# Token lists of experts 32 to 63 filled from the other end of the partitions

## The chip, the cores and the metric

The kernel runs on one core of a Trainium2 chip. Its engines are TensorE (PE, with its weight loads as PEld), VectorE (DVE), ScalarE (ACT), GpSimd (POOL) and SyncE (SP); SP, ACT and POOL also issue transfers, which sixteen DMA engines of the core carry out. The metric is the device time of one execution in microseconds, as the median of several runs.

## What is computed

One layer of a hybrid encoder on 512 tokens of width 1024: a mixer (a state space branch and a windowed attention branch), then a mixture of experts, then a norm. The change is in the routing of the mixture:

```python
scores = jax.nn.sigmoid((n @ router_w).astype(jnp.float32))
biased = scores + router_bias.astype(jnp.float32)
...
_, eidx = lax.top_k(jnp.where(emask, biased, -jnp.inf), TOP_K)
w = jnp.take_along_axis(scores, eidx, axis=-1)
w = w / jnp.sum(w, axis=-1, keepdims=True) * ROUTE_SCALE
...
for e in range(N_EXPERTS):
    hid = jax.nn.silu(n @ e_gate[e]) * (n @ e_up[e])
    out = out + (hid @ e_down[e]) * combine[:, e:e + 1]
```

There are 64 experts of hidden width 256 and one shared expert; each token goes to 6 of the 64, so 3072 rows (token and expert) are computed. All is float32.

## The kernel before

Up to about 590 us of the span the kernel does the mixer. Then the routing runs over four tiles of 128 tokens, mingled with the output projection of the mixer and with the shared expert, and from about 645 us on the experts.

**Lists.** For each token tile DVE chooses the six experts (`choose`, L1396 to L1405), PE counts with a triangular matrix how many rows of each expert came before (`positions`, L1956 and L1957), and DVE turns that into a slot for each of the six rows (`places`, L1420 to L1431). POOL then writes the entry of each row (token, weight, row number) with an indirect transfer to that slot of the table `list_d` in HBM (`list_tile`, L714, six transfers per tile; it waits for `ordered`, which `places` raises). An entry's place n in its expert's list gives its block, n / 64, and within the block its partition, 4 (n mod 16) + n / 16: sixteen entries in a row go to sixteen groups of four partitions, the next sixteen to the second partition of each group, and so on. Slots that no entry fills hold a number that is out of bounds, for which the indirect transfers move nothing. For expert 0 alone the list is also made by PE (`list_of_first`, L1448 to L1455 on DVE, L2014 on PE), so that its rows can be gathered before the table is read back. DVE then ranks the experts by length (L1484 to L1492) for the order in which they are loaded.

**Units.** The experts run in 42 units. The four first experts and the sixteen longest lists have a unit each (up to 128 rows: one block in the lower 64 partitions, one in the upper), the others share one in pairs (64 rows each, one expert per half). For each unit POOL gathers the rows of the normed tokens from HBM into `xs` (L754, one indirect transfer, one row of 4 KB per filled partition), PE turns them (L2020), ACT and DVE apply the modulation, PE does gate and up (`gate_up`, L2032), ACT and DVE the activation, PE the down product (`down`, L2040), DVE scales the result (L1510) and POOL scatters the rows to `expert_rows` in HBM (L767). PE does gate and up of a unit before the down product of the unit before.

**Weights.** An expert's weights are three transfers of 1 MB: gate (L517), up (L518) and down (L521), all issued by SP in the order of use. There are six slots. A slot's gate and up halves are loaded again when the gate and up products of the expert in it are done (`gu_ready`), its down half after its down product (`ey_ready`).

**Tail.** When all scatters have landed (L578), SP reads the six rows of each token (L582), and DVE and PE add them, DVE norms and SP stores.

On PE the order around the routing is written by hand: `shared_gu(0)`, `turn_h(3)`, `positions(2)`, part of `shared_gu(1)`, `router(3)`, the rest, `positions(3)` (waits for `choose(3)` on DVE), the row counts (L2061), `shared_gu(2, 1 to 5)`, `list_of_first` (waits for DVE's L1455), `shared_gu(2)`, `shared_turn(0)`, the ranks (L2068), `shared_gu(3)`, the turn of the first unit's rows, the rest of the shared expert, and the units. On DVE `places(2)` stands ahead of `shared_hid(0)` (L1444) and `best_two(3)` (L1378), and `places(3)` ahead of L1448. In DVE's code `chain(...)` makes the next instruction wait for the one inside.

Of the kernel before, what the change touches and what calls it, by code (L numbers as in the profile page):

```python
# [5 lines left out]
ALU = mybir.AluOpType  # L6
# [6 lines left out]
P = 128  # L13
SEQ = 512
D = 1024
T = SEQ // P
# [25 lines left out]
NE = 64  # L42
TOPK = 6
RGROUPS = 8
# [7 lines left out]
HALF = P // 2  # L52
STRIPE = 16
# [43 lines left out]
def hybrid_ssd_swa_moe_adaln_block(nc, a):  # L97
# [58 lines left out]
    with ExitStack() as ctx:  # L156
# [50 lines left out]
        with ExitStack() as own:  # L207
# [27 lines left out]
            slot = tile(own, "slot", [P, T, TOPK], U32)  # L235
# [69 lines left out]
        def dn(s):  # L305
# [24 lines left out]
        fin_g = xsT[:, 0, :, :].rearrange("p k c -> p (k c)")  # L330

        widths = [KC * NE, NE, TOPK * NE, NE, RGROUPS * 8, RGROUPS * RGROUPS, RGROUPS * RGROUPS, P, RGROUPS * RGROUPS,
                  NE, NE, NE, T * RGROUPS, T * 8, T * 8, T * TOPK, T * TOPK, P, T, T * 4, T * TOPK * 4, 2 * T * TOPK]
        routing = xsT[:, :, :, :].rearrange("p b k c -> p (b k c)")
        spans = [routing[:, sum(widths[:i]):sum(widths[:i + 1])] for i in range(len(widths))]
        r_w = spans[0].rearrange("p (k e) -> p k e", k=KC)
# [7 lines left out]
        nth_of, place0 = spans[17], spans[18]  # L344
        entry0 = spans[19].rearrange("p (t w) -> p t w", t=T)
        parts0 = spans[20].rearrange("p (t w k) -> p t w k", t=T, w=4)
        whole = spans[21].rearrange("p (t w k) -> p t w k", t=T, w=2)
        gs, top8, indf, s6, p6 = (spans[i].rearrange("p (t w) -> p t w", t=T) for i in range(12, 17))

# [680 lines left out]
        def _(dve):  # L1030
            steps = [0]

            def chain(ins):

                steps[0] += 1
                ins.then_inc(dve_step, 1)
                dve.wait_ge(dve_step, steps[0])
# [380 lines left out]
            def places(t):  # L1418
# [5 lines left out]
                dve.tensor_scalar(whole[:, t, 0, :], p6[:, t, :], -(STRIPE - 1) / 2, 1.0 / STRIPE, ALU.add, ALU.mult)  # L1424
                chain(dve.tensor_scalar(whole[:, t, 1, :], p6[:, t, :], -(HALF - 1) / 2, 1.0 / HALF, ALU.add, ALU.mult))
                dve.tensor_scalar(whole[:, t, :, :], whole[:, t, :, :], ROUND, -ROUND, ALU.add, ALU.add)
                chain(dve.scalar_tensor_tensor(out=p6[:, t, :], in0=p6[:, t, :], scalar=float(NE * HALF // STRIPE),
                                               in1=indf[:, t, 0:TOPK], op0=ALU.mult, op1=ALU.add))
                chain(dve.scalar_tensor_tensor(out=p6[:, t, :], in0=whole[:, t, 0, :], scalar=float(NE * (1 - HALF)), in1=p6[:, t, :],
                                               op0=ALU.mult, op1=ALU.add))  # L1430
                dve.scalar_tensor_tensor(out=slot[:, t, :], in0=whole[:, t, 1, :], scalar=float(NE * (HALF - HALF // STRIPE)),  # L1431
                                         in1=p6[:, t, :], op0=ALU.mult, op1=ALU.add).then_inc(ordered, 1)

            def add_shared(t):
                if t == 0:
# [752 lines left out]
```

## Time and profile before

| | us |
|---|---|
| median of 3 runs | 1208.58 |
| lowest and highest | 1207.26, 1210.27 |
| the profiled execution | 1209.25 |
| its span, first to last instruction | 1207.2 |
| PE busy | 1148.4 (95%) |
| DVE busy | 539.6 (45%) |
| POOL busy | 197.0 (16%) |
| DMA: 334.71 MB moved | mean 277 GB/s |

The span is cut into 40 slices of 30.2 us on the page of the profile. A group of instructions is named by the line of kernel.py that issued it, its engine and what it writes and reads. Idle time stands in brackets, with the engine, tile and line that ended it. The DMA share of a window is the mean of the packets' time over sixteen engines; it can be a little over 1, since packets overlap. Instructions issued by a queue's sequencer carry a q (SPq).

### The profile page before, as it was taken

To read this page: it belongs to the slowest core of one execution; us is meant where nothing else is said; L and a number is where in the kernel's file an instruction comes from. 1 tells how busy PE (TensorE), PEld (TensorE's weight loads), DVE (VectorE), ACT (ScalarE), POOL (GpSimd) and SP (SyncE) were. 2 spreads that over 40 slices of the span, in tenths; PEclk is the share of its full clock that TensorE was granted. 3 is DMA by queue.
4 is the path that set the end of the run, shared out by engine and by line. 5 is a ranking of instruction groups with operands and counts; after the bars stand their busy time and mean duration, and the time that the engine had idled before them with its cause. 6 is when DMAs were issued, how large, how long until landed. Compare 5 with 4: busy or idle time off the path is not lost. (4 is left out here: it accounts for less than half of the span.)

```text
span 1207.2 us, 13966 instructions
## 1 busy us (share of the span) xinstructions
PE 1148.4 (95%) x4935; PEld 654.0 (54%) x4935; DVE 539.6 (45%) x1160; ACT 254.6 (21%) x635; POOL 197.0 (16%) x326
## 2 busy tenths in 40 slices
PE   4999999998999999999999999999999999989885
PEld 2545875565566888889754444444444443433332
DVE  5673123555666777635764222222232222222156
ACT  2131222233442111101211111212121121111101
POOL 5000010112011010010441212121212122111101
PEclk9999999999999999999999999999999999999898
DMA  9942142233578365275447999999999999999996
GB/s 301 261 140 69 35 141 70 71 105 135 201 277 323 128 184 166 87 282 233 149 162 270 345 420 422 423 423 423 422 423 421 422 422 423 421 422 422 422 363 262
DMA packets 111212, 334.71 MB, mean 277 GB/s; under 512 B 14580, under 2 KB 67912, under 8 KB 84136
## 3 DMA queue, kind: packets, MB, share of 16 engines
q1 hardware_dynamic: 88048, 269.39, 57.4%
q0 software_dynamic: 21568, 59.68, 13.8%
q10 hardware_dynamic: 1528, 4.77, 1.0%
q8 instruction: 39, 0.64, 0.2%
q14 instruction: 29, 0.24, 0.1%
HBM read 314.51 MB, written 38.35 MB: 292 GB/s over the span
## 5 line engine op out<-in xcount | busy, mean ns | idle before, releaser
L2032 PE MATMUL ps<-gu_hi,xsT 128*64 128x512 f32 (+1 forms) x704 | 239.1, 613 | 14.5 <-DMA gu_hi<-in_exp_w_up_dram 6.9
L2032 PEld LDWEIGHTS ps<-gu_hi,xsT 128*64 128x64 f32 (+1 forms) x704 | 83.0, 154 | 124.6 <-issue 123.2
L1514 DVE SCALAR_TENSOR_TENSOR hid<-ps,wgt,gated 128x256 f32<-128x256 f32 x42 | 20.3, 483 | 280.2 <-ACT gated L1004 280.2
L2032 PE MATMUL ps<-gu_lo,xsT 128*64 128x512 f32 (+1 forms) x320 | 141.1, 594 | 1.9 <-issue 1.0
L2040 PE MATMUL ps<-dn_hi,hidT 128*64 128x512 f32 (+1 forms) x352 | 119.9, 597 | 1.1 <-DVE hn L1510 1.1
L1659 PE MATMUL ps<-n1T,ring 128*128 128x512 f32 x256 | 111.8, 593 | 0.0
L767 POOL DMA_INDIRECT expert_rows<-hn,meta x40 | 40.0, 1000 | 368.1 <-DVE hn L1510 327.7
L1510 DVE TENSOR_TENSOR hn<-ps,g_row 128x1024 f32<-128x1024 f32 x42 | 51.4, 1224 | 91.0 <-PE ps L2040 90.8
L1004 ACT ACTIVATE gated<-ps 128x256 f32<-128x256 f32 x42 | 16.1, 384 | 306.1 <-PE ps L2032 306.1
L1659 PEld LDWEIGHTS ps<-n1T,ring 128*128 128x128 f32 x256 | 48.2, 190 | 58.4 <-issue 58.4
L2032 PEld LDWEIGHTS ps<-gu_lo,xsT 128*64 128x64 f32 (+1 forms) x320 | 49.9, 161 | 51.9 <-issue 51.6
L2040 PE MATMUL ps<-dn_lo,hidT 128*64 128x512 f32 (+1 forms) x160 | 72.5, 596 | 0.0
L994 ACT ACTIVATE xsT<-ps,mod 128x128 f32<-128x128 f32 x172 | 64.8, 457 | 27.8 <-PE ps L2020 27.8
L2040 PEld LDWEIGHTS ps<-dn_hi,hidT 128*64 128x64 f32 (+1 forms) x352 | 38.7, 150 | 48.1 <-issue 46.2
L1504 DVE TENSOR_SCALAR xsT<-ps,mod 128x128 f32<-128x128 f32 x172 | 58.7, 403 | 6.5 <-PE ps L2020 6.5
L2020 PEld LDWEIGHTS ps<-ident,hn 128*128 128x128 f32 x344 | 42.9, 191 | 30.5 <-issue 27.5
L1844 PE MATMUL ps<-xbcT,ring 128*128 128x512 f32 x128 | 58.4, 599 | 0.0
L1668 PE MATMUL ps<-ring,n1T 128*128 128x256 f32 x256 | 57.6, 386 | 0.0
L1924 PE MATMUL ps<-ring,raw 128*128 128x256 f32 x256 | 56.6, 380 | 0.9 <-issue 0.9
L1668 PEld LDWEIGHTS ps<-ring,n1T 128*128 128x128 f32 x256 | 49.1, 193 | 7.5 <-issue 0.7
L1924 PEld LDWEIGHTS ps<-ring,raw 128*128 128x128 f32 x256 | 48.1, 190 | 7.5 <-issue 1.2
L754 POOL DMA_INDIRECT hn<-norm_rows,meta x44 | 46.1, 1047 | 34.5 <-issue 32.1
(387 smaller groups left out, 1531.1 us busy)
## 6 DMA issues: line engine op xcount, KB each, us to landing
gu_hi<-in_exp_w_gate_dram SPq DMA_DIRECT2D x44, 1024.0 KB, 25.4
gu_hi<-in_exp_w_up_dram SPq DMA_DIRECT2D x44, 1024.0 KB, 28.8
dn_hi<-in_exp_w_down_dram SPq DMA_DIRECT2D x44, 1024.0 KB, 28.9
ring<-in_w_in_dram SPq DMA_DIRECT2D x20, 1024.0 KB, 6.1
gu_lo<-in_exp_w_gate_dram SPq DMA_DIRECT2D x20, 1024.0 KB, 26.2
gu_lo<-in_exp_w_up_dram SPq DMA_DIRECT2D x20, 1024.0 KB, 29.6
dn_lo<-in_exp_w_down_dram SPq DMA_DIRECT2D x20, 1024.0 KB, 29.5
h<-in_ada_w_dram POOLq DMA_DIRECT2D x32, 512.0 KB, 4.9
```

The lines of the kernel that those rows point to most:

```text
L754: pool.indirect_dma_start(out=xs[:, b, :], out_offset=None, in_=norm_d[:, :], in_offset=bass.IndirectOffsetOnAxis(ap=meta[:, c, 0:1], axis=0),
L767: pool.indirect_dma_start(out=rows_d[:, :], out_offset=bass.IndirectOffsetOnAxis(ap=meta[:, c, 1:2], axis=0), in_=ys[:, b, :], in_offset=N ...
L994: ins = act.activation(xsT[:, b, k, :], ps[:, 0, P * k:P * k + P], ACT.Identity, bias=B2[:, k:k + 1], scale=A2[:, k:k + 1])
L1504: ins = dve.tensor_scalar(xsT[:, b, k, :], ps[:, 1, P * (k - 4):P * (k - 4) + P], A2[:, k:k + 1], B2[:, k:k + 1], ALU.mult, ALU.add)
L1510: dve.tensor_tensor(ys[:, b, :], flat(ps[:, 5:7, :]), g2_row[:, :], ALU.mult).then_inc(ey_dve, 1)
L1659: ins = pe.matmul(bank, w[:, k, lo:lo + P], n1T[:, k, :], start=(k == 0), stop=(k == KC - 1))
L1668: ins = pe.matmul(bank[:, 0:cols], n1T[:, k, P * t:P * t + P], w[:, k, :], start=(k == 0), stop=(k == KC - 1))
L1844: ins = pe.matmul(ps[:, 1, :], w[:, k, P * (m % 2):P * (m % 2) + P], uT[:, k, :], start=(k == 0), stop=(k == KC - 1))
L1924: ins = pe.matmul(ps[:, 2 * (t % 2) + b // 2, WB * (b % 2):WB * (b % 2) + WB], mergedT[:, k, P * t:P * t + P], w[:, k, :], start=(k == 0), ...
L2020: ins = pe.transpose(ps[:, k // 4, P * (k % 4):P * (k % 4) + P], xs[:, b, :].rearrange("p (f k) -> p k f", k=KC)[:, k, :], ident[:, :])
L2032: ins = pe.matmul(ps[rows, 2 + b, :], xsT[:, b, k, rows], gu(s)[:, :, k, :], start=(k == 0), stop=(k == KC - 1))
L2040: ins = pe.matmul(ps[rows, 5 + half, :], hidT[:, jj, rows], dn(s)[:, jj, BANK * half:BANK * half + BANK], start=(jj == 0), stop=(jj == 1))
```

## The change

The slots of experts 32 to 63 are mirrored within each half of 64 partitions: an entry that went to partition p of its block goes to 63 - p. The slot is p x 64 + e + 4096 x block; the old code made it with three instructions out of the place, the two rounded quotients (`whole`: place / 16 and place / 64) and the expert's number. The new code forms the partition with a factor of 1 or -1 (`turned_round`, first a mask of experts from 32 up) and adds a base (`base_of`) that is the expert's number for the others and includes the far end of the block for the turned ones. Six instructions more per token tile, all on 128 x 6 elements.

```diff
-                  NE, NE, NE, T * RGROUPS, T * 8, T * 8, T * TOPK, T * TOPK, P, T, T * 4, T * TOPK * 4, 2 * T * TOPK]
+                  NE, NE, NE, T * RGROUPS, T * 8, T * 8, T * TOPK, T * TOPK, P, T, T * 4, T * TOPK * 4, 2 * T * TOPK, TOPK, TOPK]
...
+        turned_round, base_of = spans[22], spans[23]
...
                 dve.tensor_scalar(whole[:, t, :, :], whole[:, t, :, :], ROUND, -ROUND, ALU.add, ALU.add)
-                chain(dve.scalar_tensor_tensor(out=p6[:, t, :], in0=p6[:, t, :], scalar=float(NE * HALF // STRIPE),
-                                               in1=indf[:, t, 0:TOPK], op0=ALU.mult, op1=ALU.add))
-                chain(dve.scalar_tensor_tensor(out=p6[:, t, :], in0=whole[:, t, 0, :], scalar=float(NE * (1 - HALF)), in1=p6[:, t, :],
-                                               op0=ALU.mult, op1=ALU.add))
-                dve.scalar_tensor_tensor(out=slot[:, t, :], in0=whole[:, t, 1, :], scalar=float(NE * (HALF - HALF // STRIPE)),
-                                         in1=p6[:, t, :], op0=ALU.mult, op1=ALU.add).then_inc(ordered, 1)
+                chain(dve.tensor_scalar(turned_round, indf[:, t, 0:TOPK], float(NE // 2), None, ALU.is_ge))
+                dve.tensor_scalar(base_of, whole[:, t, 1, :], float(2 * HALF * NE), float((HALF - 1) * NE), ALU.mult, ALU.add)
+                chain(dve.scalar_tensor_tensor(out=p6[:, t, :], in0=whole[:, t, 0, :], scalar=-float((HALF - 1) * STRIPE) / HALF,
+                                               in1=p6[:, t, :], op0=ALU.mult, op1=ALU.add))
+                dve.tensor_tensor(base_of, base_of, turned_round, ALU.mult)
+                chain(dve.scalar_tensor_tensor(out=p6[:, t, :], in0=whole[:, t, 1, :], scalar=float(STRIPE - 1),
+                                               in1=p6[:, t, :], op0=ALU.mult, op1=ALU.add))
+                dve.tensor_tensor(base_of, base_of, indf[:, t, 0:TOPK], ALU.add)
+                chain(dve.tensor_scalar(turned_round, turned_round, -2.0, 1.0, ALU.mult, ALU.add))
+                chain(dve.tensor_tensor(p6[:, t, :], p6[:, t, :], turned_round, ALU.mult))
+                dve.scalar_tensor_tensor(out=slot[:, t, :], in0=p6[:, t, :], scalar=float(NE * HALF // STRIPE), in1=base_of,
+                                         op0=ALU.mult, op1=ALU.add).then_inc(ordered, 1)
```

DVE, places(3), before. `xsT` is the buffer in which all small routing tiles lie; `dve_step` is the semaphore of `chain`, `counted` is raised by PE.

```order
L1420 TENSOR_TENSOR xsT<-dn_hi,ps 128x384 [waits counted]
L1423 TENSOR_REDUCE xsT<-xsT 128x6 [waits dve_step]
L1424 TENSOR_SCALAR xsT<-xsT 128x6 [waits dve_step]
L1425 TENSOR_SCALAR xsT<-xsT 128x6
L1426 TENSOR_SCALAR xsT<-xsT 128x12 [waits dve_step]
L1427 SCALAR_TENSOR_TENSOR xsT<-xsT 128x6
L1429 SCALAR_TENSOR_TENSOR xsT<-xsT 128x6 [waits dve_step]
L1431 SCALAR_TENSOR_TENSOR slot<-xsT 128x6 [waits dve_step]
L1448 SCALAR_TENSOR_TENSOR xsT<-ps,dn_hi 128x4
```

The same place after the change, from the rounding on (lines are up to seven higher from here on):

```order
L1427 TENSOR_SCALAR xsT<-xsT 128x12 [waits dve_step]
L1428 TENSOR_SCALAR xsT<-xsT 128x6
L1429 TENSOR_SCALAR xsT<-xsT 128x6 [waits dve_step]
L1430 SCALAR_TENSOR_TENSOR xsT<-xsT 128x6
L1432 TENSOR_TENSOR xsT<-xsT 128x6 [waits dve_step]
L1433 SCALAR_TENSOR_TENSOR xsT<-xsT 128x6
L1435 TENSOR_TENSOR xsT<-xsT 128x6 [waits dve_step]
L1436 TENSOR_SCALAR xsT<-xsT 128x6
L1437 TENSOR_TENSOR xsT<-xsT 128x6 [waits dve_step]
L1438 SCALAR_TENSOR_TENSOR slot<-xsT 128x6 [waits dve_step]
L1455 SCALAR_TENSOR_TENSOR xsT<-ps,dn_hi 128x4
```

Three instructions have become nine, five of the nine wait for the one before, and the write of `slot` stands last in both.

PE, from positions(3) to the first matmul of `shared_gu(3)`, is the same sequence in both kernels; so it reads before:

```order
L1956 MATMUL ps<-xsT,ones 128x64 [waits ordered,routed]
L1957 MATMUL ps<-dn_hi,xsT 128x64
L2061 MATMUL ps<-xsT,ones 128x64 [waits score_done]
L2061 MATMUL ps<-dn_hi,ones 128x64
L1979 MATMUL ps<-gu_hi 128x512 [waits n2_dve,shared_in]
L1979 MATMUL ps<-gu_hi 128x512 x4
L2014 MATMUL ps<-xsT,lists 128x4 [waits o_read,list0_in]
...
L2068 MATMUL ps<-dn_hi,ecol 1x64 [waits routed]
L1979 MATMUL ps<-gu_hi 128x512 [waits ordered,shared_in]
```

Nothing moved there, but three of these waits (`ordered` and `routed` at the first row, `list0_in`, `routed` at L2068) are for DVE instructions that stand behind the changed step.

## Rows read from the trace of the kernel before

**Rows 1.** Page: busy time and share per engine; busy tenths in 40 slices.
```profile
PE 1148.4 (95%) x4935; PEld 654.0 (54%) x4935; DVE 539.6 (45%) x1160; ACT 254.6 (21%) x635; POOL 197.0 (16%) x326
DMA  9942142233578365275447999999999999999996
```

**Rows 2.** Windows: start and end, length, busy per engine, granted clock, DMA share, GB/s.
```profile
617.40:626.70 9.30, 9.30 (x26) 4.34 (x27) 2.42 (x14) 0.66 (x2) 5.91 (x7) 1.00 0.07 14
645.00:650.00 5.00, 5.00 (x13) 2.25 (x12) 2.33 (x2) 0.00 (x0) 0.00 (x0) 1.00 0.56 210
650.00:655.00 5.00, 3.70 (x18) 2.13 (x19) 2.05 (x7) 2.17 (x6) 0.31 (x2) 1.00 0.44 131
660.00:665.00 5.00, 5.00 (x23) 2.50 (x20) 1.85 (x5) 1.89 (x5) 0.00 (x0) 1.00 0.46 166
665.00:1148.00 483.00, 467.19 (x1811) 202.94 (x1809) 129.65 (x315) 89.09 (x235) 94.45 (x159) 0.99 1.02 417
800.00:1146.00 346.00, 333.85 (x1298) 144.73 (x1296) 90.59 (x221) 63.30 (x167) 66.74 (x113) 0.98 1.02 422
```

**Rows 3.** Waits of PE, 690 to 1165 us: total, times, longest; and one such wait.
```profile
PE ps L2032 <- DMA gu_hi<-in_exp_w_up_dram: 7.8, 3, 3.6
PE ps L2032 <- DMA gu_lo<-in_exp_w_up_dram: 3.9, 2, 3.1
...
1118.71 9.65 PE L2032 MATMUL ps<-gu_hi,xsT 128*64 128x512 f32 x32 [3.64 <-DMA gu_hi<-in_exp_w_up_dram]
```

**Rows 4.** Chain that ended last, in order of time: start, length, what.
```profile
1024.29 8.78 PE ps L2032 x32
...
1046.31 29.30 DMA gu_hi<-in_exp_w_up_dram
...
1106.31 27.73 DMA gu_hi<-in_exp_w_up_dram
...
1134.37 7.09 PE ps L2032 x32
...
1148.94 8.75 DMA expert_rows<-hn,meta
...
1157.75 0.34 SPq L582
```

**Rows 5.** Windows at the end of the weight stream, columns as in rows 2.
```profile
1146.00:1148.00 2.00, 0.56 (x4) 0.32 (x2) 1.45 (x3) 0.38 (x1) 0.00 (x0) 1.00 1.02 430
1148.00:1150.00 2.00, 0.34 (x2) 0.23 (x4) 0.00 (x0) 0.00 (x0) 1.06 (x2) 1.00 0.95 401
1150.00:1152.00 2.00, 2.00 (x12) 0.86 (x10) 0.00 (x0) 0.00 (x0) 1.24 (x3) 1.00 0.93 391
1152.00:1154.00 2.00, 2.00 (x12) 0.71 (x10) 0.00 (x0) 0.00 (x0) 0.08 (x1) 1.00 0.79 322
1154.00:1156.00 2.00, 2.00 (x12) 0.84 (x10) 0.00 (x0) 0.00 (x0) 0.00 (x0) 1.00 0.65 258
1156.00:1158.00 2.00, 2.00 (x14) 1.16 (x12) 0.61 (x2) 0.51 (x2) 0.00 (x0) 1.00 0.38 154
1158.00:1160.00 2.00, 2.00 (x12) 0.61 (x10) 1.24 (x4) 1.38 (x4) 0.00 (x0) 1.00 0.77 197
1160.00:1162.00 2.00, 1.86 (x10) 0.57 (x6) 0.46 (x1) 0.11 (x1) 0.00 (x0) 1.00 0.98 406
```

**Rows 6.** Timeline of DVE, places(3): start, length, engine, line, operation.
```profile
614.05 0.17 DVE L1424 TENSOR_SCALAR xsT<-xsT 128x6 f32<-128x6 f32 x1
614.13 0.16 DVE L1425 TENSOR_SCALAR xsT<-xsT 128x6 f32<-128x6 f32 x1
614.33 0.17 DVE L1426 TENSOR_SCALAR xsT<-xsT 128x12 f32<-128x12 f32 x1
614.41 0.16 DVE L1427 SCALAR_TENSOR_TENSOR xsT<-xsT 128x6 f32<-128x6 f32 x1
614.60 0.17 DVE L1429 SCALAR_TENSOR_TENSOR xsT<-xsT 128x6 f32<-128x6 f32 x1
614.80 0.17 DVE L1431 SCALAR_TENSOR_TENSOR slot<-xsT 128x6 uint32<-128x6 f32 x1
```

**Rows 7.** Timeline of DVE: what stands behind places(0) and places(1).
```profile
575.23 0.69 DVE L1351 TENSOR_TENSOR work<-ps,g_row 128x512 f32<-128x512 f32 x1 [2.52 <-PE ps L1924]
...
592.16 0.69 DVE L1351 TENSOR_TENSOR work<-ps,g_row 128x512 f32<-128x512 f32 x1 [2.60 <-PE ps L1924]
```

**Rows 8.** Timeline, tile 2's slots to the stream's start; window; gather's time to landing.
```profile
605.27 0.17 DVE L1431 SCALAR_TENSOR_TENSOR slot<-xsT 128x6 uint32<-128x6 f32 x1
605.35 0.42 DVE L1444 TENSOR_TENSOR lists<-ps,gated 128x256 f32<-128x256 f32 x1
605.68 0.21 DVE L1378 TENSOR_TENSOR xsT<-dn_hi,xsT 128x64 f32<-128x64 f32 x1
606.27 1.01 POOL L714 DMA_INDIRECT token_lists<-pay,slot  x1 [2.04 <-DVE slot L1431]
607.59 0.97 POOL L714 DMA_INDIRECT token_lists<-pay,slot  x1 [0.30 <-issue]
...
611.32 0.43 PE L1956 MATMUL ps<-xsT,ones 128*128 128x64 f32 x2 [0.58 <-DVE dn_hi L1405]
...
615.80 1.06 POOL L714 DMA_INDIRECT token_lists<-pay,slot  x1 [1.94 <-DVE slot L1431]
...
616.55 0.97 PEld L2014 LDWEIGHTS ps<-xsT,lists 128*128 128x128 f32 x8 [0.61 <-DVE xsT L1455]
...
619.89 1.05 POOL L754 DMA_INDIRECT hn<-norm_rows,meta  x1 [0.48 <-issue]
...
626.76 1.04 PE L2020 MATMUL ps<-ident,hn 128*128 128x128 f32 x8
...
644.68 7.03 PE L2032 MATMUL ps<-gu_hi,xsT 128*128 128x512 f32 x16
...
651.89 0.33 SPq L517 DMA_DIRECT2D gu_hi<-in_exp_w_gate_dram  x1
...
661.66 0.33 SPq L517 DMA_DIRECT2D gu_hi<-in_exp_w_gate_dram  x1
...
DMA to landing us min/median/max: 3.1/9.6/17.0
...
626.70:651.60 24.90, 24.90 (x98) 12.98 (x97) 14.30 (x30) 2.83 (x8) 5.51 (x8) 1.00 0.76 284
```

## The prediction

> **What bounds the kernel now.** I read the page of the profile first: its row of busy times says 95% for PE, and the row of the DMA engines stands at nine tenths from the middle of the span to its end [rows 1]. So two resources look full in the expert part, and the windows tell them apart. From 665 to 1148 us the DMA share is 1.02, which is what full looks like in this view; before that, at 645 to 655 and 660 to 665 us, it is 0.44 to 0.56, because the six weight slots are full and the next load must wait until PE has freed one [rows 2]. The table of waits has PE waiting 7.8 + 3.9 us for expert weights [rows 3], and the chain of waits runs over PE until 1044 us and then over two weight loads that take 29.30 and 27.73 us from issue to landing [rows 4]. A transfer of 1 MB at 422 GB/s is 2.5 us; such a load stands behind some ten others. PE has small gaps, the transfers none: from 665 us on the time is set by how much the DMA engines have to move, and by when the stream starts. The stream starts when PE has used the first expert, so PE's and DVE's time before 652 us counts, and almost nothing that PE, DVE, ACT or POOL do between 665 and 1134 us does.
>
> "The DMA engines" are sixteen, and a load has landed when the last of them is done. The windows at the stream's end show that they don't end together: the share falls from 1.02 to 0.95, 0.93, 0.79, 0.65 and 0.38 between 1148 and 1158 us, while the last scatter of rows, issued at 1148.94, lands only at 1157.69, and SP issues the reads of the tail right behind it, at 1157.75 [rows 4, 5]. Below full by 0.07, 0.09, 0.23, 0.37 and 0.64, times 2 us: the mean engine is idle for 2.8 us there. With the next two windows (0.77 and 0.98, in part the start of the new reads) it is 3.4 us. So the busiest engine ends some 2.8 to 3.4 us after the mean one, and the tail waits for the busiest.
>
> **The change, part by part: the DVE work.** It keeps three of the six instructions behind the reduction at L1423 and puts nine in the place of the other three, six more per tile. What matters is the distance of two starts. On tile 3 an instruction that waits for the one before starts 0.19 or 0.20 us after it (614.13 to 614.33, 614.41 to 614.60, 614.60 to 614.80) and one that waits for nothing 0.08 us after (614.05 to 614.13) [rows 6]. From L1426 to the write of slot that is 0.08 + 0.19 + 0.20 = 0.47 us. In the new order the starts behind the rounding are 0.08 (turned_round), 0.19 (base_of), 0.08, 0.20, 0.08, 0.20, 0.08, 0.20, 0.20 = 1.31 us. So +0.84 us for each tile.
>
> Which tiles pay? Tiles 0 and 1 end in front of an idle DVE: it waits 2.52 and 2.60 us there for the output projection [rows 7]. That covers 0.84, and POOL's list writes of these tiles are behind a queue of their own (1.3 us from start to start [rows 8], six per tile). Behind tile 2 DVE goes on at once with L1444 and L1378, and both what it reads there are ready; POOL waits for the slots of tile 2 (2.04 us) and again for those of tile 3 (1.94 us), and PE waits for DVE at positions(3), 0.58 us, and before list_of_first, 0.61 us [rows 8]. These are waits that end with DVE, so the delay passes on: 0.84 us at positions(3) and 1.68 us at list_of_first. Queued behind the waiting matmul are the shared expert, the turn of the first gathered rows and the first unit, and PE is busy without a gap from 617.4 to 651.6 us [rows 2, 8], so nothing there takes the delay up. Nor does a transfer: the DMA share is 0.07 between 617.4 and 626.7 us [rows 2]. The first gather has landed by then (POOL issues it at 619.89, and the 3.1 us that such a gather takes at the least [rows 8] are over before PE's turn at 626.76; both move alike). SP's loads into freed slots, issued at 651.89 and 661.66 us [rows 8], move with PE. The stream starts **1.7 us later**. Ends: 0, if something else ends these waits, and 4 x 0.84 = 3.4 us if all four tiles pay. I take 1.7, for the idle time in rows 7 is three times the addition and there is none behind tiles 2 and 3.
>
> **The balance.** A list's n-th entry of a block goes to partition 4 (n mod 16) + n/16 of its half; entries without a token move no row. Lists are 3 to 125 entries long on these inputs (by the reference's routing), and 60 of the 64 end within a round of 16, which leaves the higher groups of four partitions one row short. Summed over all units, the 32 groups of four partitions hold between 76 and 110 rows, mean 96; with the lists of experts 32 to 63 turned they hold between 91 and 100. A row is 4 KB and is moved twice, gathered and scattered. At 422 GB/s over sixteen engines 4 KB take 4096 / 26.4 = 155 ns [rows 2]. If an engine serves fixed partitions, one group's 14 rows above the mean are 14 x 2 x 0.155 = 4.3 us of work, and 4 rows are 1.2 us. The idle time of the tail, 2.8 to 3.4 us, is of that size, which is why I believe that it comes from the rows. The turned lists take (14 - 4)/14 = 0.71 of the excess away: 0.71 x 3.1 = **2.2 us sooner**. Ends: 0, if engines do not serve fixed partitions or their lag has another cause, and 3.4 us, all that the tail shows idle.
>
> The Trainium skill ("DMA: Bandwidth & Descriptors", section "The descriptor swizzle") states which engine writes which partitions: groups g and g+8 of a half belong to one engine. By that pairing the busiest engine has 208 rows against a mean of 192 now, and 198 then; an estimate from it is 10 x 2 x 0.155 = 3.1 us sooner, and the sum would be 1.7 - 3.1 = -1.4 us, 1207.2 us.
>
> **The sum.** The profiled execution took 1209.25 us, 1207.2 of it the span; the median of the runs is 0.67 us lower. +1.7 - 2.2 = -0.5 us: 1208.75 us for a profiled execution, 1208.1 us against the median of 1208.58. What is late next is the same engine as before: after the change the stream is still full, its last load and the last scatter still end it, and the 13 MB of reads behind it and the tail on DVE do not change.
>
> **Rivals.** (1) The cost is hidden: PE's two waits of 0.6 us are ended by something that doesn't move, or the start of the stream is set by a transfer. The nearly idle DMA engines of 617.4 to 626.7 us speak against it. 1208.58 - 2.2 = 1206.4. (2) The balance is worth nothing: all engines share one limit, and those that end first only had the smaller share. For it: the share is 1.02 whatever runs. Against it: the staircase in rows 5, with 16 equal parts in every weight load. 1208.58 + 1.7 = 1210.3. (3) Slower: the engines that serve the highest partitions are slow by themselves, and their short lists hid it. The turned lists give a high group of four 13 to 16 rows more; 13 x 2 x 0.155 = 4.0 us on that engine, and with 1.7 us of DVE 5.7 us: 1214.3. It decides as soon as that engine's own slowness is over 13 rows' worth, 4 us in 490. Rows 5 show one long staircase and no engine's name, so nothing excludes it; little speaks for it. The Trainium skill (the same page, section "Latency and other measured facts") has such a rule: engines 7 and 15 are "usually slower" than the others. By its swizzle these serve the highest groups of the two halves. No row here names an engine, so no run here shows it. (4) More than the tail: PE's stalls go too. A stall is followed by slow matmuls: behind the 3.64 us wait at 1118.71 the 32 matmuls take 9.65 us in place of 7.1 [rows 3, 4]. If that stall and its slow stretch go and PE, not the stream, then sets the last scatter, 3.6 + 2.6 us go and 1.7 us come: 1204.1. Against it: PE is given its time back only where it is the later of the two, and at 1134.37 it again waits for a load.
>
> **How the numbers follow.** Chances: the forecast 0.55 (1206.5 to 1209.7 us, the gain between 1.4 and 3.4 us and the cost between 1.4 and 2.4), rival 1 0.12, rival 2 0.13, rival 3 0.10, rival 4 0.10. The range reaches from the largest gain at no cost, 1208.58 - 3.4 = 1205.2, to no gain at the cost of four tiles with a small margin for the runs' own spread, 1211.8; outside stay rivals 3 and 4. A measurement of this kernel tells about 0.3%, 3.6 us, from no change. Faster by more than that: rival 4 and a small part of rival 1, 0.12. Slower: rival 3 and a small part of rival 2, 0.12. Within: 0.76.
>
> **What the profile after would show.** In the places step of tiles 2 and 3 the distance from L1427 to the write of slot is 1.3 us, and the first unit's L2032 (now L2039) starts near 646.4 us in place of 644.68. The first load into a freed slot is issued near 653.6 us. The DMA share is 1.02 until about 1150 us and then falls in one or two windows, not in five; the idle time summed over these windows is near 1 us in place of 2.8 to 3.4. The last scatter lands near 1157.2. I am wrong in the cost if the first unit starts within 0.5 us of its old time, and wrong in the gain if the staircase is gone and the last scatter still lands later than 1158.5, or if the staircase is as long as it was.

## The result, and the profile after

| | before | changed |
|---|---|---|
| median of 11 runs each, same chip | 1208.89 | 1212.40 |
| lowest and highest | 1205.95, 1210.27 | 1208.76, 1213.23 |
| ratio, with 95% interval | | 1.0022 [1.0014, 1.0031] |
| the profiled execution and its span | 1209.25, 1207.2 | 1208.76, 1206.6 |

The change costs 2.7 us by the ratio (1.7 to 3.7); the medians stand 3.5 us apart. 2.7 us is less than the 3.6 us that this kernel's measurement tells from no change, so by size it is the case "within 0.3%"; but the interval excludes a gain, and 1212.4 lies above the range that I gave.

The profiled execution of the changed kernel happens to be the quickest of its eleven. Its part ahead of the changed code ran 2.2 us earlier: the first matmul of the output projection stands at 527.96 us before and at 525.72 after, at the same code. So absolute times of the two traces are not to be compared; what is compared here is the distance from one event to a later one.

First the DVE work. The timeline of DVE in the changed kernel, places(3) (start, length, engine, line, operation), answers to [rows 6]:

```profile
612.90 0.17 DVE L1427 TENSOR_SCALAR xsT<-xsT 128x12 f32<-128x12 f32 x1
612.98 0.16 DVE L1428 TENSOR_SCALAR xsT<-xsT 128x6 f32<-128x6 f32 x1
613.18 0.17 DVE L1429 TENSOR_SCALAR xsT<-xsT 128x6 f32<-128x6 f32 x1
...
614.01 0.17 DVE L1437 TENSOR_TENSOR xsT<-xsT 128x6 f32<-128x6 f32 x1
614.21 0.17 DVE L1438 SCALAR_TENSOR_TENSOR slot<-xsT 128x6 uint32<-128x6 f32 x1
```

From the rounding to the write of `slot` it is 1.31 us, against 0.47. The waits around it in the changed kernel, timelines of DVE, PE, POOL and SP, answer to [rows 7, 8]:

```profile
573.02 0.69 DVE L1352 TENSOR_TENSOR work<-ps,g_row 128x512 f32<-128x512 f32 x1 [1.69 <-PE ps L1931]
...
604.86 1.01 POOL L715 DMA_INDIRECT token_lists<-pay,slot  x1 [2.11 <-DVE slot L1438]
...
609.90 0.43 PE L1963 MATMUL ps<-xsT,ones 128*128 128x64 f32 x2 [1.62 <-DVE dn_hi L1406]
...
651.28 0.33 SPq L518 DMA_DIRECT2D gu_hi<-in_exp_w_gate_dram  x1
```

DVE's idle time behind tile 0 has shrunk from 2.52 to 1.69 us, by just the addition: there it is hidden. PE's wait for DVE at positions(3) has grown from 0.58 to 1.62 us. The write of the first slots (571.16 us) comes 1.38 us earlier than before, the first load into a freed slot only 0.61 us earlier (651.28 against 651.89), and the part ahead of both is 2.24 us earlier: 1.63 us are lost on the way.

So from the first matmul of the output projection to the first load into a freed slot it is 123.93 us before and 125.56 after.

Then the stream's end. Windows of the changed kernel, columns as in [rows 2], answering to [rows 5]:

```profile
1148.00:1150.00 2.00, 0.43 (x2) 0.23 (x4) 0.00 (x0) 0.00 (x0) 1.18 (x3) 1.00 1.02 430
1150.00:1152.00 2.00, 2.00 (x12) 0.86 (x10) 0.00 (x0) 0.00 (x0) 1.19 (x3) 1.00 0.98 412
1152.00:1154.00 2.00, 2.00 (x12) 0.81 (x10) 0.00 (x0) 0.00 (x0) 0.00 (x0) 1.00 0.83 336
1154.00:1156.00 2.00, 2.00 (x12) 0.75 (x10) 0.00 (x0) 0.00 (x0) 0.00 (x0) 1.00 0.48 180
1156.00:1158.00 2.00, 2.00 (x14) 1.16 (x12) 0.70 (x2) 0.60 (x2) 0.00 (x0) 1.00 0.57 131
1158.00:1160.00 2.00, 2.00 (x12) 0.70 (x10) 1.15 (x4) 1.29 (x4) 0.00 (x0) 1.00 0.84 332
```

The staircase is shorter at its top: the share stands at 0.98 until 1152, so the engines that used to be done first now work longer. It is not gone: the share still falls to 0.48. And the last weight load lands when it did. The group of the last load's issue, before and then changed (the time to landing is that of the last of sixteen engines):

```profile
L521 SPq DMA_DIRECT2D dn_lo<-in_exp_w_down_dram x1: 498/498/498, 1133.5 to 1133.5; - x1
...
DMA to landing us min/median/max: 26.2/26.2/26.2
```

```profile
L522 SPq DMA_DIRECT2D dn_lo<-in_exp_w_down_dram x1: 679/679/679, 1133.2 to 1133.2; - x1
...
DMA to landing us min/median/max: 26.4/26.4/26.4
```

1133.5 + 26.2 = 1159.7 us before and 1133.2 + 26.4 = 1159.6 after, though the stream started 0.6 us earlier: 507.8 us after the first load into a freed slot before, 508.3 us after it now. The last scatter of rows landed 505.8 us after that load before and 505.1 us now (at 1156.35 us). The chain of waits of the changed kernel no longer goes over it, but over the last up load and PE:

```profile
1118.01 31.22 DMA gu_lo<-in_exp_w_up_dram
1149.57 7.09 PE ps L2039 x32
1157.74 3.61 PE ps L2047 x16
1161.73 24.14 DMA gu_hi<-expert_rows
```

**A measure for all runs.** Each of these loads raises its semaphore sixteen times, and the trace holds those times; I take them for the landings on the sixteen engines. From them I took, for the last down load of each kernel, the mean of the sixteen landings and how far the first and the last stand from it. The column "start" is the distance from the first matmul of the output projection to the first load into a freed slot, "behind" the distance from that load to the end of the span. The table is mine, not a view of the profile; "foretold" is explained with the experiments.

```
kernel           first freed   start    behind   mean landing   first    last     rows, fullest    foretold
                 slot's load                     after that     engine   engine   engine (of 192)  last engine
before           651.89        123.93   555.3    504.1          -7.2     +3.7     208              +4.3
changed          651.28        125.56   555.3    504.0          -3.5     +4.3     198              +4.8
same_again       654.93        126.36   555.3    504.1          -3.4     +4.1     198              +4.8
none_turned      653.45        125.53   555.8    504.0          -7.7     +3.9     208              +4.3
all_turned       653.63        125.53   557.9    503.3          -7.5     +5.2     207              +4.8
early_only       651.81        123.89   555.5    504.0          -7.3     +3.4     208              +4.3
rotated_4        650.64        123.94   558.1    503.5          -5.0     +7.3     208              +8.0
rotated_15       652.08        123.95   554.1    504.1          -4.3     +2.7     207              +3.7
two_rotations    649.76        123.95   554.5    504.1          -4.3     +2.1     204              +2.4
unstriped        652.26        124.18   564.5    504.8          -8.6     +11.8    247              +15.1
no_rows_half_pe  647.65        120.49   494.8    445.7          -2.0     +2.0     0
```

The mean landing comes 504 us after the stream's start in every kernel that moves all rows (503.3 to 504.8): the work is the same. What the balance of rows can change is how far the last engine lags behind the mean. In the changed kernel the first engine moved from 7.2 us ahead to 3.5, and the last one stayed nearly where it was, 4.3 against 3.7. The two columns in front say where the time went: the kernels with nine instructions in all four tiles start 1.6 us later (same_again 2.4), and behind the start the changed kernel takes as long as the one before.

### The profile page after: what moved, and what is told of

It reads as the page before. It is cut to its first block and busy times, and to the rows that moved or that the text cites. A ratio compares the mean times of both kernels' runs of the same rounds, so it can differ in the third digit from the quotient of the medians.

```text
span 1206.6 us, 13990 instructions
## 1 busy us (share of the span) xinstructions
PE 1146.0 (95%) x4935; PEld 653.4 (54%) x4935; DVE 542.8 (45%) x1184; ACT 254.6 (21%) x635; POOL 197.4 (16%) x326
## 5 line engine op out<-in xcount | busy, mean ns | idle before, releaser
L1666 PEld LDWEIGHTS ps<-n1T,ring 128*128 128x128 f32 x256 | 48.2, 190 | 58.4 <-issue 58.4
L1851 PE MATMUL ps<-xbcT,ring 128*128 128x512 f32 x128 | 58.4, 599 | 0.0
```

The source lines that it names most:

```text
L1666: ins = pe.matmul(bank, w[:, k, lo:lo + P], n1T[:, k, :], start=(k == 0), stop=(k == KC - 1))
L1851: ins = pe.matmul(ps[:, 1, :], w[:, k, P * (m % 2):P * (m % 2) + P], uT[:, k, :], start=(k == 0), stop=(k == KC - 1))
```

## Experiments: the price of the DVE work

**none_turned.** The nine instructions, with a mask that never applies, so every slot is as before:

```diff
-                chain(dve.tensor_scalar(turned_round, indf[:, t, 0:TOPK], float(NE // 2), None, ALU.is_ge))
+                chain(dve.tensor_scalar(turned_round, indf[:, t, 0:TOPK], float(NE), None, ALU.is_ge))
```

> The changed kernel with its mask never true (experts from 64 up): the nine DVE instructions and the old slots. Theory A (the DVE work costs 1.7 us, and the turned lists gave nothing or cost a little): 1208.9 + 1.7 = 1210.6 us, the tail of the DMA share as in the kernel before. Theory B (the DVE work explains all of the loss, the turning nothing): the same time as the changed kernel, 1212. Theory C (the loss is from the turned lists): within 1 us of the kernel before.

Measured 1210.98 us, ratio to the kernel before 1.0015 [1.0004, 1.0026]: +1.8 us. The staircase is the old one; windows of this kernel:

```profile
1150.00:1152.00 2.00, 0.68 (x2) 0.32 (x4) 0.00 (x0) 0.00 (x0) 1.32 (x3) 0.79 0.94 397
1152.00:1154.00 2.00, 2.00 (x8) 0.62 (x6) 0.00 (x0) 0.00 (x0) 1.04 (x1) 0.50 0.89 375
1154.00:1156.00 2.00, 2.00 (x12) 0.66 (x10) 0.00 (x0) 0.00 (x0) 0.00 (x0) 0.85 0.79 318
1156.00:1158.00 2.00, 2.00 (x12) 0.74 (x10) 0.00 (x0) 0.00 (x0) 0.00 (x0) 1.00 0.55 215
1158.00:1160.00 2.00, 2.00 (x11) 0.52 (x7) 0.00 (x0) 0.00 (x0) 0.00 (x0) 1.00 0.36 143
```

By the medians' ratio the DVE work alone is two thirds of the loss. The interval reaches from 0.5 to 3.1 us, so by itself it tells none of the three theories from the others; the trace does for theory C: the stream starts 1.60 us later (125.53 against 123.93 us), of the forecast size, with the old slots.

**early_only.** The same nine instructions for token tiles 0 and 1, the old three for 2 and 3:

```diff
+                if t < 2:
+                    chain(dve.tensor_scalar(turned_round, indf[:, t, 0:TOPK], float(NE), None, ALU.is_ge))
...
+                else:
+                    chain(dve.scalar_tensor_tensor(out=p6[:, t, :], in0=p6[:, t, :], scalar=float(NE * HALF // STRIPE),
```

> The nine instructions with a mask that never applies (so the slots are those of before) for token tiles 0 and 1 only; tiles 2 and 3 have the old three. Theory (the idle DVE behind tiles 0 and 1 hides the 0.84 us of each): no change, 1208.8. Rival (all tiles pay, the cost in the changed kernel is spread over four): +0.8 to +1.7 us, 1209.6 to 1210.5.

Measured 1209.12 us, ratio 0.9997 [0.9988, 1.0006]. Twelve of the 24 added instructions cost nothing that can be measured, which leaves the cost to the others. The column "start" says the same: 123.89 us, against 123.93 before.

**same_again.** The changed kernel once more, beside none_turned and all_turned on their chip:

> The changed kernel again, on the same chip as the others and with a second profile. Every theory: near 1212 us. Theory A and C: slower than none_turned by 1 to 2 us or more; theory B: equal to it.

Measured 1211.65 us, ratio 1.0024 [1.0014, 1.0035], +2.9 us, the same as the first time. Against none_turned the median is 0.7 us higher, with intervals that overlap: at the same DVE work, the better balance brought no gain that the runs can show.

Its trace shows a second price of the delay. Counted from the output projection, its stream starts 0.8 us later than in the changed kernel's first trace. All of that comes in PE's matmuls right behind the longer wait at positions(3), at a granted clock of about half:

```profile
612.72 0.43 PE L1963 MATMUL ps<-xsT,ones 128*128 128x64 f32 x2 [1.64 <-DVE dn_hi L1406]
...
614.00:616.00 2.00, 2.00 (x4) 0.80 (x3) 1.83 (x8) 0.00 (x0) 0.97 (x1) 0.53 0.03 2
616.00:618.00 2.00, 2.00 (x5) 0.73 (x4) 1.82 (x11) 0.00 (x0) 0.00 (x0) 0.62 0.00 0
```

The traces of changed, none_turned and all_turned have the longer wait too and a clock of 1.00 there; the kernel before, with a wait of 0.58 us, also has 1.00. How often the clock falls in the runs, no run here shows.

## Experiments: what the balance of rows does

**all_turned.** The mask always applies (threshold 0.0 in the same line), so all lists but that of the first unit fill from the other end; the spread between engines is that of before, mirrored.

> The same instructions with a mask that is always true: all lists filled from the far end. By the number of rows alone the load of the groups of partitions is the mirror image of the kernel before (76 to 110 rows in a group), so the time is that of none_turned within 0.5 us. If the engines that serve the high partitions are slow by themselves, these now have the most rows: 4 us or more above none_turned, 1214 or more, and a longer staircase at the end of the stream.

Measured 1212.77 us, ratio 1.0031 [1.0019, 1.0044], +3.7 us, 1.8 us more than none_turned with overlapping intervals. It fits none of the theories well. High groups that are slow by themselves, rival 3 of the prediction, asked for 4 us or more over none_turned. The last engine is at +5.2 us, against +3.9, and the stretch behind the start is 2.1 us longer; the fit below makes the last engine only 0.5 us later. What the rest is stays open.

**no_rows.** The kernel before, in which both bounds of the indirect transfers are 0, so that only token 0's rows and row 0 are moved; the rest of the expert part computes on what stands in the buffers:

```diff
-            last_token, last_row = pool.to_reg(SEQ - 1), pool.to_reg(NROW - 1)
+            last_token, last_row = pool.to_reg(0), pool.to_reg(0)
```

> The kernel before with both bounds of the indirect transfers at 0, so that all rows but row 0 are left out of gather and scatter (the expert part computes on stale data). What is left of the unevenness of the sixteen engines is not from the number of rows. If the rows make it: the DMA share falls from full to nothing within one window of 2 us at the stream's end. If the engines differ by themselves: a staircase of 3 us or more stays. The weights alone are 201 MB, so the stream should end some 20 MB / 422 GB/s = 50 us sooner, unless PE is the bound then.

Measured 1184.56 us in one run. A window of this kernel shows why it can't answer the question that it was made for:

```profile
800.00:1100.00 300.00, 300.00 (x1173) 130.91 (x1173) 84.09 (x205) 58.77 (x155) 60.43 (x102) 1.00 0.94 377
```

PE is busy in all of it and the DMA share is 0.94: without the rows PE is the bound, and the engines stay together: the sixteen landings of the last down load stand within 1.8 us. It settles another point, that PE's bound lies some 24 us below the stream's.

**no_rows_half_pe.** So the same again, with gate and up over only half of their contraction, which takes PE out of the way:

```diff
-                for k in range(KC):
+                for k in range(KC // 2):
                     for rows, s in parts(slots):
                         ins = pe.matmul(ps[rows, 2 + b, :], xsT[:, b, k, rows], gu(s)[:, :, k, :],
-                                        start=(k == 0), stop=(k == KC - 1))
+                                        start=(k == 0), stop=(k == KC // 2 - 1))
```

> No rows are gathered or scattered (both bounds 0) and gate and up take only half of their contraction, so that PE is no longer the bound and the stream of weights runs with full engines and without any rows of tokens. It shows whether the engines drift apart by themselves over the stream. Theory A: the last loads land on sixteen engines spread over several us (some 2 to 5 us from first to last), the share falls off in two windows or more. Rival B: within 1 us of each other.

Measured 1144.79 us in one run. Now the stream is full; windows of the stream and of its end:

```profile
700.00:1080.00 380.00, 312.58 (x1197) 138.60 (x1197) 115.22 (x280) 79.61 (x210) 83.57 (x141) 0.94 1.02 418
...
1088.00:1090.00 2.00, 2.00 (x10) 0.73 (x8) 0.00 (x0) 0.00 (x0) 0.00 (x0) 0.87 1.00 410
1090.00:1092.00 2.00, 2.00 (x14) 1.16 (x12) 0.63 (x2) 0.53 (x2) 0.00 (x0) 1.00 0.99 381
1092.00:1094.00 2.00, 2.00 (x12) 0.63 (x10) 1.22 (x4) 1.36 (x4) 0.00 (x0) 1.00 0.97 369
```

The windows show next to no staircase here (the tail's reads are already there to fill it), so that part of what I expected was wrong. The landings do show it: the last down load's sixteen stand from 2.0 us ahead of the mean to 2.0 us behind, where the first ones of the stream stand within 2.0 us in all. Four engines are 1.4 to 2.0 us ahead, six 1.0 to 2.0 us behind. No rows of tokens are moved in this kernel, so **the engines drift apart without them**. The first engine's lead grows with the stream, from 0.4 us for the loads near 700 us to 1.0 us near 850 and 2.0 us at the end; the last one's lag is 1.5 us at the start, falls to 0.9 and ends at 2.0. The run gives the price of a row as well: the mean landing comes 445.7 us after the stream's start in place of 504.1, and 58.4 us over 192 rows for each engine is 0.304 us for a row gathered and scattered; 2 x 0.155 = 0.31 was the forecast.

**The fit behind the next three.** I took the sorted landings of every down load in the first five traces (before, changed, same_again, none_turned, all_turned) and fitted them by two terms: 0.16 us for each row that an engine has moved, and an own lag for each of sixteen engines that grows evenly over the stream. Which partitions an engine serves I took from the Trainium skill ("DMA: Bandwidth & Descriptors", section "The descriptor swizzle"): groups of four partitions g and g + 8 of a half belong to one engine. With rows alone the error is 0.60 to 0.93 us (root mean square) in the five traces under that assignment; with sixteen blocks of eight partitions in order it is 1.59 and 1.50 for before and none_turned (0.72 and 0.66, better, for the changed kernel's two), and with the partition modulo 16 it is 11.9 for before. With the own lags it is 0.43 to 0.48. By the fit, in us against the mean at the stream's end:

```
engine's first group of a half     0     1     2     3     4     5     6     7
lower 64 partitions             -2.1  -0.2  -0.4  +2.4  +2.9  +0.9  +0.6  -2.4
upper 64 partitions             -2.5  -0.6  -1.0  +1.1  +1.5  +1.0  +1.2  -2.3
```

By it four engines are 2.1 to 2.5 us ahead, the middle ones behind. The landings carry no engine's name, only their order, so the five traces alone do not fix which engine has which lag: fitted again with a simpler count of the rows moved so far, other assignments come out as well (0.64 against 0.65 us). With early_only, rotated_4, rotated_15 and two_rotations added, over the last eight down loads, the assignment above is the best that 300 random starts found, 0.29 us against 0.35 for the next. "Foretold" in the table above is the largest sum of own lag and 0.32 us for each row above 192. A fit with sixteen free terms can please itself, so the next kernels were made to be foretold by it. They change no slot and no DVE instruction, only which partition each row of the list table is read to.

**rotated_4** and **rotated_15.** All groups of a half are moved up by four, or by fifteen, for all units but the first, whose list PE makes; the same rows, on other engines, and the fullest engine has 208 and 207 of them. For rotated_4:

```diff
-            pool.dma_start(lo[:, 0:2, :], list_v[:, 0:2, :]).then_inc(lists_in, 16)
-            pool.dma_start(hi[:, 0:2, :], list_v[:, 0:2, :]).then_inc(lists_in, 16)
-            pool.wait_ge(lists_in, 32)
+            for to in (lo, hi):
+                pool.dma_start(to[16:HALF, 0:2, :], list_v[0:HALF - 16, 0:2, :]).then_inc(lists_in, 16)
+                pool.dma_start(to[0:16, 0:2, :], list_v[HALF - 16:HALF, 0:2, :]).then_inc(lists_in, 16)
+            pool.wait_ge(lists_in, 64)
```

> The old slots and the old DVE code. Only the read of the token lists from HBM into the SBUF is changed: table row p of a block goes to partition (p + 16) mod 64 of its half, so that the sixteen groups of four partitions stand rotated by four; two more reads of lists on POOL, ahead of the gather of unit 1, which has some 10 us to spare (POOL waits 12.3 us for PE afterwards). The same rows are moved, and the busiest group of four holds as many as before. Theory A (the sixteen DMA engines differ by themselves: fitted to the landings of the five traces, the ones that carry groups 3 and 4 of a half lag some 2.5 us behind the mean, those of groups 0 and 7 lead by 2.3): the fullest groups now fall on the lagging engines, 0.32 us per row: the last engine ends 8.0 us behind the mean in place of 4.3, +3.7 us, about 1212.5 where before has 1208.8. Rival B (only the busiest engine's number of rows counts, engines are alike): the same as before within 0.5 us, 1208.8. Rival C (the balance does not reach the time): also no change, and no longer staircase either.

> As the one before, rotated by fifteen groups (partition (p + 60) mod 64), which puts the two fullest groups of each half on the engines that theory A has as light. Theory A: the last engine ends 3.7 us behind the mean, -0.6 us against before, 1208.2, and 4.3 us less than rotated by four. Rivals B and C: no change, and no difference from rotated by four.

Measured 1212.26 us (ratio 1.0035 [1.0022, 1.0048]) and 1208.23 us (0.9995 [0.9986, 1.0003]), where 1212.5 and 1208.2 were expected. The two differ by 4 us in the median, and by 4.0 us in the stretch behind the start, and in nothing but where the same rows lie. The fit's error on their landings, which it had not seen, is 0.48 and 0.47 us, and 0.81 and 0.74 without the own lags. Windows at the end of the stream, first rotated_4, then rotated_15:

```profile
1150.00:1152.00 2.00, 0.59 (x4) 0.36 (x6) 0.00 (x0) 0.00 (x0) 1.25 (x4) 0.98 0.78 324
1152.00:1154.00 2.00, 2.00 (x8) 0.69 (x6) 0.00 (x0) 0.00 (x0) 0.93 (x1) 0.50 0.57 221
1154.00:1156.00 2.00, 2.00 (x8) 0.71 (x6) 0.00 (x0) 0.00 (x0) 0.00 (x0) 0.67 0.35 145
1156.00:1158.00 2.00, 2.00 (x12) 0.84 (x10) 0.00 (x0) 0.00 (x0) 0.00 (x0) 1.00 0.26 102
```

```profile
1150.00:1152.00 2.00, 2.00 (x7) 0.61 (x4) 0.00 (x0) 0.00 (x0) 0.64 (x1) 0.54 1.00 418
1152.00:1154.00 2.00, 2.00 (x8) 0.78 (x6) 0.00 (x0) 0.00 (x0) 0.00 (x0) 0.61 0.93 369
1154.00:1156.00 2.00, 2.00 (x12) 0.86 (x10) 0.00 (x0) 0.00 (x0) 0.00 (x0) 1.00 0.63 252
1156.00:1158.00 2.00, 2.00 (x12) 0.69 (x8) 0.00 (x0) 0.24 (x1) 0.00 (x0) 1.00 0.70 201
```

One staircase is deeper than that of before, the other begins later and ends at 0.63. Both have a stretch at a lower granted clock (0.50 to 0.67), in which the last unit's gate and up take 8.8 us in place of 7.09; as it stands in both, it does not explain their difference. The rival that only counts the rows of the fullest engine, and the one by which the balance does not reach the time at all, both fall here.

**unstriped.** The list's n-th entry of a block stands in partition n, by eight reads in place of two:

```diff
+            list_s = list_d.rearrange("(b j i e) w -> i j b (e w)", b=NBLK, j=STRIPE, i=HALF // STRIPE)
+            for to in (lo, hi):
+                for i in range(HALF // STRIPE):
+                    pool.dma_start(to[STRIPE * i:STRIPE * i + STRIPE, 0:2, :], list_s[i, :, 0:2, :]).then_inc(lists_in, 16)
```

> The old slots and DVE code; the read of the lists undoes the stripes, so that the n-th entry of a block stands in partition n. Eight reads of lists in place of two (some 4 us more on POOL ahead of the gather of unit 1, covered). By the pairing of groups the busiest engine then has 247 rows against 208 before (mean 192). Rows on an engine cost time (A and B): at 0.32 us for a row gathered and scattered +10.8 us by A (lag 15.1 against 4.3), +12.5 us by B, so 1219.6 to 1221.3. Theory C (all engines share one limit, the balance does not matter): no change, 1208.8.

Measured 1218.94 us, ratio 1.0092 [1.0078, 1.0107], +11.1 us. Its windows fall off from 1148 us on and reach the bottom eight windows later:

```profile
1148.00:1150.00 2.00, 2.00 (x12) 0.86 (x10) 0.00 (x0) 0.00 (x0) 0.00 (x0) 1.00 0.85 342
...
1156.00:1158.00 2.00, 1.20 (x6) 0.31 (x2) 1.12 (x1) 0.38 (x1) 0.00 (x0) 1.00 0.43 180
...
1164.00:1166.00 2.00, 2.00 (x12) 0.68 (x9) 0.00 (x0) 0.15 (x1) 0.00 (x0) 1.00 0.22 88
```

The last engine lags 11.8 us, 8.1 more than before, with 39 rows more on the fullest engine. The stripes that the kernel already had are worth this much; in what they left, row counts and own lags are of one size. The fit foretold 15.1, too much: by 1000 us the first engines are 10 us ahead and the loads that wait for a slot hold them back, which it does not know.

**two_rotations.** An attempt at a kernel that beats both: the middle engines get the fewest rows. In the lower half the lists of experts 0 to 31 are rotated by five groups and the others by seven, in the upper half all by seven.

```diff
+            for to, cols, by in ((lo, slice(0, 2 * NE), 20), (lo, slice(2 * NE, 4 * NE), 28), (hi, slice(0, 4 * NE), 28)):
+                pool.dma_start(to[by:HALF, 0:2, cols], list_v[0:HALF - by, 0:2, cols]).then_inc(lists_in, 16)
+                pool.dma_start(to[0:by, 0:2, cols], list_v[HALF - by:HALF, 0:2, cols]).then_inc(lists_in, 16)
```

> The old slots and DVE code; only the read of the token lists is changed, as in the rotated kernels: in the lower 64 partitions the lists of experts 0 to 31 are rotated by five groups and those of 32 to 63 by seven, in the upper 64 all by seven, with six reads in place of two (2 to 3 us more on POOL, covered as in the rotated kernels). It gives the engines that carry the middle groups the fewest rows and costs no DVE instruction. Theory A (rows at 0.32 us each plus each engine's own lag, as fitted before and as it foretold the two rotations): the last engine ends 2.4 us behind the mean in place of 4.3, -1.9 us, 1206.9, faster than both kernels. Rival (the engine's own lag isn't tied to the engine, the rotations' difference came from something else): the busiest engine has about as many rows as before, 1208.8.

Measured 1208.33 us against 1208.62, ratio 0.9999 [0.9990, 1.0008]. The stream did nearly as foretold: the last engine lags 2.1 us (2.4 foretold, 3.7 before). The time did not: a gain of 1.9 us lies outside the interval, one of 1 us inside, and the stretch behind the start is 0.8 us shorter. Its chain of waits:

```profile
1115.05 30.66 DMA gu_lo<-in_exp_w_up_dram
1146.05 9.85 PE ps L2033 x32
1156.99 3.61 PE ps L2041 x16
1161.45 24.18 DMA gu_hi<-expert_rows
```

The last unit's gate and up take 9.85 us in place of 7.09, since PE's granted clock was 0.50 (the lower of its two levels, 1.2 GHz) from 1146 to 1150 us behind a wait of 3.3 us for the last up load. From the last weight load's landing to the end it is 48.2 us, 47.5 before; so of the 1.5 us that the stream gained in this trace, 0.7 came back behind it. That the slow clock took them isn't shown: same_again has such a stretch too (8.78 us in place of the changed kernel's 7.09), and both take 555.3 us behind the start. Whether the rest is real this measurement can't tell. I don't call it faster.

## Why the prediction was wrong

**What bounds the kernel** was right: the mean landing came 504 us after the first freed slot's load in all kernels that move all rows, whatever PE or DVE did, and PE's waits for weights, 10.4 + 3.1 us in the changed kernel against 7.8 + 3.9 [rows 3], without effect.

**The DVE cost** was right in size and place: 0.84 us for a tile (1.31 - 0.47, measured 0.84), tiles 2 and 3 alone. Forecast 1.7, measured 1.63 us in the trace (1.60 in none_turned and all_turned, 2.43 in same_again) and 1.8 us by none_turned's ratio; early_only confirms the half that is free. Rival 1 (cost hidden) is out.

**The balance** is the step that failed: "The idle time of the tail, 2.8 to 3.4 us, is of that size, which is why I believe that it comes from the rows. The turned lists take (14 - 4)/14 = 0.71 of the excess away". Two errors are in it. The idle time summed over the windows is the mean engine's lead over the last one. I took that lead for the work of the group with the most rows. But the fullest engine (208 rows, 16 above the mean, 5.1 us) is by the fit one of those that run 2.1 us ahead by themselves, so it ends only 3.0 us behind the mean. By the fit three engines end last before, 4.2 to 4.3 us behind: that of groups 1 and 9 of the lower half, which had 206 rows and has 195 now, and the two middle ones of that half, which had 198 and 196 rows and have 196 and 198 now. Of the middle ones' lag 2.4 and 2.9 us are their own, and the change touches neither that nor, in sum, their rows; they still end last. And agreement of size between 4.3 us of row excess and 3.1 us of idle time was all that linked the two; nothing in [rows 5] named an engine. In place of a gain of 2.2 us the last engine ends 0.6 us later (3.7 to 4.3; 0.4 in same_again), and behind the start of the stream the time is the same, 555.3 us.

**The sum.** By the traces the loss is 1.6 us ahead of the first freed slot's load and nothing behind it, and in same_again 2.4 and nothing; the last engine's 0.6 us do not show in that stretch. The ratios say 2.7 and 2.9 us, both from 1.7 us up; a part of what is missing may be such executions as same_again's, with 0.8 us at the lower clock behind PE's longer wait, a term that the prediction did not have; their number isn't known. The range was also narrower than its description: no gain at the cost of four tiles is 1208.58 + 3.4 = 1212.0 us, and 1211.8 was written. Nearest was rival 2 (the balance is worth nothing, 1210.3), and for a wrong reason: it said that the engines share one limit, while unstriped and rotated_4 cost 11.1 and 4.2 us (by their ratios) by the balance alone. Rival 3 had the right kind of cause, engines that differ by themselves, at the wrong place. It set the high groups as slow; by the fit the engines that serve groups 7 and 15 of a half are among the quickest. The Trainium skill's rule behind it ("DMA: Bandwidth & Descriptors", section "Latency and other measured facts", engines 7 and 15 usually slower) is not borne out by these runs: by the fit, with the engines named by the Trainium skill's swizzle, these two end 2.4 and 2.3 us ahead of the mean. The estimate from the Trainium skill's swizzle, 3.1 us sooner, had the right assignment and failed for the same reason as mine.

**The signs that I had named**: the first unit's start and the first load moved as said once the 2.2 us ahead of them are taken off (1.64 and 1.63 us later, 1.7 forecast). The signs of the gain did not come: the share was to fall in one or two windows with an idle time near 1 us, and it falls over three (0.98, 0.83, 0.48) before the new reads raise it; summed as in the prediction, over the windows up to 1160 us, the idle time is 2.8 us. That was nearly the second condition for being wrong in the gain, a staircase as long as it was.

What stays open: why the middle engines lag. No run here shows the cause, only that the sixteen drift apart without rows too, to 2 us each way in 446 us, and that it matters on which partitions the rows lie. How much of two_rotations' shorter stream reaches the median is also open, and how often the clock falls behind PE's longer wait.

## What to carry to other kernels

When a transfer ends with the last of sixteen engines, the staircase of the DMA share tells how far the last one lags, unless later transfers fill it, but not why; find out which engine is last before its load is evened out, by moving the same rows to other partitions, which here cost nothing on DVE. By the fit, rows laid on engines that run ahead are free up to their lead, so an even count is not the optimum; rotated_15 and two_rotations shortened the stretch behind the start by 1.2 and 0.8 us in one trace each, and the medians don't show it. And an addition of small dependent instructions is priced by the distance of their starts (0.20 us when one waits for the one before, 0.08 when not), on the tiles behind which the engine has no idle time.

## What the runs showed of the hardware

- The sixteen DMA engines did not run alike on equal shares. After 446 us of a full stream of weights they stood 4.0 us apart, from first to last; by the fit over the longer stream 5.4 us, with the same four ahead in both halves (groups 0 and 7).
- No evening out between the engines shows in the traces: the tail's first read, issued at 1157.37 us in rotated_4, 4.1 us ahead of the last engine's last weights, landed 6.6 us later, 2.5 us after them; in rotated_15 it took 5.1 us, again 2.5 us after them, and before and in the changed kernel 4.9 and 5.7 us, 3.0 and 2.5 us after them.
- A row of 4 KB gathered and scattered cost its engine 0.304 us in a full stream (the mean over sixteen engines, from one run without rows).
